# Conditioning chunks 5 to 24 computed between the projection units of layer 0

## The reference

```
mod     = silu(c)     @ ada_w[i] + ada_b[i]      # 1 x 6144, ada_w[i] is 1024 x 6144
mod_ctx = silu(c_ctx) @ ada_w[i] + ada_b[i]
sh1, sc1, gt1, sh2, sc2, gt2 = split(mod, 6)
z = modulate(rmsnorm(x, pre_mix_g), sh1, sc1) @ w_in       # 1024 x 1888
...                                                        # three mixers (MLA, pooling, RWKV-7), w_out
x = x + gt1 * rmsnorm(y, post_mix_g)
h = modulate(rmsnorm(x, pre_ffn_g), sh2, sc2)              # then the MoE, 64 experts
x = x + gt2 * rmsnorm(f, post_ffn_g)
```

## Time and profile before

| | us |
|---|---|
| median of 3 runs (lowest, highest) | 2706.94 (2706.51, 2714.57) |
| the profiled execution, time | 2704.16 |
| its span, first to last instruction | 2702.3 |
| TensorE busy | 2199.4 (81%) |
| VectorE busy | 866.5 (32%) |
| mean granted clock of TensorE | 0.904 |

### The profile page before, as it was taken

How to read it: one execution, slowest core, us unless ns; L and a number is a source line. 1 busy time by engine, 2 the same in 40 slices (tenths; PEclk the granted TensorE clock), 3 DMA queues, 4 the chain that set the end, 5 groups by cost and what they waited for, 6 DMA issues and landing times. The chain is left out here.

```text
span 2702.3 us, 40433 instructions
## 1 busy us (share of the span) xinstructions
PE 2199.4 (81%) x15579; PEld 1215.5 (45%) x15579; DVE 866.5 (32%) x1930; ACT 347.5 (13%) x716; POOL 382.8 (14%) x563
## 2 busy tenths in 40 slices
PE   7999888778866888888996497877775999899990
PEld 1124465666435444444443244566533444444440
DVE  0220146675472111111111632567543111111113
ACT  0001232110220011011110013211020111111110
POOL 0000100000100222222221101000001222222220
PEclk9999989997976999899998699799786999999995
DMA  9890100003104999999994811000305999999983
GB/s 337 310 324 9 46 1 1 2 2 129 48 16 181 380 377 376 352 389 358 382 379 182 327 54 47 1 2 3 138 23 217 386 375 373 383 378 370 369 317 118
DMA packets 150297, 571.69 MB, mean 212 GB/s; under 512 B 26327, under 2 KB 36439, under 8 KB 116248
## 3 DMA queue, kind: packets, MB, share of 16 engines
q1 hardware_dynamic: 125600, 532.14, 51.9%
q0 software_dynamic: 24576, 37.82, 4.1%
HBM read 569.75 MB, written 46.24 MB: 228 GB/s over the span
## 5 line engine op out<-in xcount | busy, mean ns | idle before, releaser
L1137 PE MATMUL pb<-arena 128*64 128x256 f32 x3072 | 353.0, 380 | 15.1 <-DMA arena<-in_exp_w_down_dram 14.7
L1134 PE MATMUL pb<-arena 128*128 128x512 f32 x512 | 270.0, 686 | 98.8 <-DMA arena<-in_exp_w_down_dram 96.3
L1137 PEld LDWEIGHTS pb<-arena 128*64 128x64 f32 x3072 | 214.5, 134 | 135.7 <-issue 35.9
L1938 DVE TENSOR_TENSOR arena<-arena,pb 128x128 f32<-128x128 f32 (+1 forms) x128 | 41.1, 321 | 691.2 <-ACT arena L1403 691.2
L1982 POOL TENSOR_TENSOR arena<-arena 128x8 f32<-128x8 f32 (+1 forms) x44 | 74.7, 1698 | 1132.9 <-DVE arena L1439 643.3
L698 PE MATMUL pb<-arena 128*128 128x128 f32 x1136 | 156.2, 281 | 94.9 <-DVE arena L1447 68.0
L1134 PEld LDWEIGHTS pb<-arena 128*128 128x128 f32 x512 | 109.7, 220 | 239.1 <-issue 234.7
L720 PE MATMUL pb<-arena 128*128 128x480 f32 (+1 forms) x512 | 207.1, 566 | 2.3 <-ACT arena L1220 2.3
L698 PEld LDWEIGHTS pb<-arena 128*128 128x128 f32 x1136 | 127.8, 144 | 156.7 <-issue 152.8
L1152 PE MATMUL pb<-arena 128*64 128x512 f32 x768 | 186.0, 604 | 1.5 <-DVE arena L1944 1.5
L690 PE MATMUL pb<-arena 128*2 128x512 f32 x384 | 169.3, 602 | 18.8 <-DMA arena<-in_ada_w_dram 18.8
(11 more groups left out here) (291 smaller groups left out, 2678.1 us busy)
## 6 DMA issues: line engine op xcount, KB each, us to landing
arena<-in_exp_w_gate_dram SPq DMA_DIRECT2D x128, 1024.0 KB, 9.7
arena<-in_exp_w_up_dram SPq DMA_DIRECT2D x128, 1024.0 KB, 12.2
arena<-in_exp_w_down_dram SPq DMA_DIRECT2D x128, 1024.0 KB, 17.0
arena<-in_ada_w_dram SPq DMA_DIRECT2D x24, 2048.0 KB, 9.1
arena<-y_rows SPq DMA_DIRECT2D x36, 512.0 KB, 6.0
arena<-mod_rows SPq DMA_DIRECT2D x21, 512.0 KB, 8.5
arena<-in_w_out_dram SPq DMA_DIRECT2D x8, 1024.0 KB, 8.4
arena<-in_w_in_dram SPq DMA_DIRECT2D x4, 1920.0 KB, 16.8
```

The costliest lines, as they stand in the source:

```text
L1134: last = mm(pb[:, 2 + j % 2, :], gT[:, j % 2, k, :], ring_gu[:, j, :, k, :], start=(k == 0), stop=(k == KD - 1))
L1137: last = mm(pb[f * FEW:(f + 1) * FEW, 2 + j % 2, 0:FF], gT_few[:, j % 2, k, :], ring_gu[:, j, :, k, f * P:(f + 1) * P], start=(k == 0), st ...
```

## The change

Only the rows sh1 and sc1 of layer 0 (four chunks, in the order 2, 3, 0, 1) are computed ahead of the projection, from four buffers of their own. `w_in` of layer 0 is loaded right behind them. The other 20 chunks are loaded one at a time into the space of `mix`, in two halves of 1 MB, and multiplied behind the units of layer 0's projection, 5 chunks for every 4 units (`ada_after`). A chunk's products no longer accumulate in one pair of rows: k-slice k goes to the column group k mod 4, 32 columns wide (2 used, the others zero), so that four partial sums stand at partitions 0, 32, 64 and 96. ScalarE copies the 128 x 512 bank to SBUF, and one more matmul with a 0/1 matrix (`fold`) adds the four. VectorE then makes the finished half row of the chunk (`mod_add`), with the gain where there is one, and it is stored on its own: by ScalarE's queue for the first four, which also issues the four broadcast loads, by SyncE for the others. Squares and roots of all four token tiles of layer 0 are made at once, ahead of the first norm. The MLA weights of layer 0 are loaded when the last row is stored. All tile turns use banks 0 and 1, since 2 and 3 hold the partial sums.

```diff
+    parts["fold"] = (t[:, None] % 32) == np.arange(2)[None, :]
...
+        first_ada = Region(arena, R0, R2).take(4 * KD * 512).rearrange("p (j k n) -> p j k n", j=4, k=KD)
+        ada_ring = mix.rearrange("p i d -> p (i d)").rearrange("p (h k n) -> p h k n", h=2, k=4)
...
+        mod_row = r.take(4 * 512).rearrange("p (j n) -> p j n", j=4)
+        gain_row = r.take(512)
...
+        ADA = [(0, c) for c in (2, 3, 0, 1, 4, 5, 6, 7, 8, 9, 10, 11)] + [(1, c) for c in (2, 3, 0, 1, 4, 5, 6, 7, 8, 9, 10, 11)]
+        N_ADA = len(ADA)
+        ada_after = lambda n: range(4 + n * (N_ADA - 4) // (4 * NT), 4 + (n + 1) * (N_ADA - 4) // (4 * NT))
...
+            return {1: "pre_mix_g", 2: "post_mix_g", 4: "pre_ffn_g", 5: "post_ffn_g"}.get(ADA[n][1] // 2)
...
+                l, c = ADA[n]
+                own = slice(c * 512, (c + 1) * 512)
+                sp.dma_start(mod_row[0:2, n % 4, :], A["ada_b"][l:l + 1, own].broadcast_to([2, 512])).then_inc(ada_rows_in, 16)
+                if ada_gain(n):
+                    of = slice(c % 2 * 512, (c % 2 + 1) * 512)
+                    sp.dma_start(ada_gain_at(n), A[ada_gain(n)][l:l + 1, of].broadcast_to([2, 512])).then_inc(ada_rows_in, 16)
...
+            def mod_store(q, n):
+                l, c = ADA[n]
+                q.wait_ge(ada_row, n + 1)
+                q.dma_start(mod_dram[l][:, c * 512:(c + 1) * 512], mod_row[0:2, n % 4, :]).then_inc(mod_out, 16)
+            def ada_stream(chunks):
+                for n in chunks:
+                    l, c = ADA[n]
+                    w = A["ada_w"][l].rearrange("(p k) n -> p k n", p=P)[:, :, c * 512:(c + 1) * 512]
+                    for h in range(2):
+                        sp.wait_ge(ada_part, 2 * n - 1 + h)
+                        sp.dma_start(ada_ring[:, h], w[:, 4 * h:4 * h + 4, :]).then_inc(ada_in[h], 16)
+                    if n > chunks[0]:
+                        mod_store(sp, n - 1)
+                    sp.wait_ge(mod_out, 16 * n)
+                    ada_rows(n)
+            def ada_last(n):
+                mod_store(sp, n)
+                sp.wait_ge(mod_out, 16 * (n + 1))
...
-            for n in range(12 * DEPTH):
-                l, c = n // 12, n % 12
-                if n >= NA:
-                    sp.wait_ge(ada_sum, n + 1 - NA)
-                sp.dma_start(ada_ring[:, n % NA], A["ada_w"][l].rearrange("(p k) n -> p k n", p=P)[:, :, c * 512:(c + 1) * 512]
-                             ).then_inc(ada_in[n % NA], 16)
...
-                        load_bc(0, 1)
-            for c in range(4):
+            sp.dma_start(cst, A["shape_consts"]).then_inc(start_in, 16)
+            for n in range(4):
+                l, c = ADA[n]
+                sp.dma_start(first_ada[:, n], A["ada_w"][l].rearrange("(p k) n -> p k n", p=P)[:, :, c * 512:(c + 1) * 512]).then_inc(ada_in[n], 16)
+                ada_rows(n)
+            sp.dma_start(x[:, 0:NL, :], A["x"].rearrange("a (i p) d -> p (a i) d", p=P)).then_inc(tokens_in, 16)
+            load_w_in(0, 0)
+            sp.dma_start(x[:, NL:NT, :], A["ctx"].rearrange("a (i p) d -> p (a i) d", p=P)).then_inc(tokens_in, 16)
+            for c in range(1, 4):
                 load_w_in(0, c)
-            mod_store(DEPTH - 1)
+            ada_stream(range(4, N_ADA))
+            ada_last(N_ADA - 1)
...
+                    g = k % 4
+                    last = mm(pb[32 * g:32 * g + 32, 2 + n % 2, :], cs[:, k, :], w[:, g, :], start=(k < 4), stop=(k >= 4))
+                return last
+            def ada_main(n):
+                pe.wait_ge(ada_row, n - 1)
+                for h in range(2):
+                    pe.wait_ge(ada_in[h], 16 * (n - 2))
+                    ada_products(n, ada_ring[:, h], range(4 * h, 4 * h + 4)).then_inc(ada_part, 1)
+            def ada_fold(n):
+                pe.wait_ge(ada_copy, n + 1)
+                mm(pb[0:2, 2 + n % 2, :], c_("fold"), mod_part[:, n % 2, :], start=True, stop=True).then_inc(ada_sum, 1)
...
-            pe.wait_ge(ada_row, 12 * DEPTH)
+            for n in range(4):
+                if n >= 2:
+                    pe.wait_ge(ada_row, n - 1)
+                pe.wait_ge(ada_in[n], 16)
+                ada_products(n, first_ada[:, n, 0:4, :], range(4)).then_inc(ada_part, 1)
+                ada_products(n, first_ada[:, n, 4:8, :], range(4, 8)).then_inc(ada_part, 1)
+                if n == 0:
+                    pe.wait_ge(start_in, 16)
+                else:
+                    ada_fold(n - 1)
+            ada_fold(3)
+            pe.wait_ge(ada_row, 4)
...
                     pe.wait_ge(h_ready, seen(h_ready))
-                    turn_tile(hbuf[:, i % 2, :], 2 * (i % 2)).then_inc(hT_sum, 1)
...
                         n += 1
                         if c == 2 and i + 1 < NT:
                             h_turn(i + 1)
+                        for a in ada_after(n - 1) if l == 0 else ():
+                            ada_main(a)
+                            if a > 4:
+                                ada_fold(a - 1)
+                if l == 0:
+                    ada_fold(N_ADA - 1)
+                    pe.wait_ge(ada_row, N_ADA)
...
+            act.wait_ge(cs_zero, 1)
+            ac(cs[:, :, 0:2].rearrange("p k s -> p s k"), craw, ACT.Silu).then_inc(silu_c, 1)
+            def ada_copied(n):
+                act.wait_ge(ada_part, 2 * n + 2)
+                if n >= 2:
+                    act.wait_ge(ada_sum, n - 1)
+                ac(mod_part[:, n % 2, :], pb[:, 2 + n % 2, :], ACT.Copy).then_inc(ada_copy, 1)
+            for n in range(4):
+                ada_copied(n)
+            for n in range(4):
+                act.wait_ge(ada_row, n + 1)
+                act.dma_start(mod_dram[0][:, ADA[n][1] * 512:(ADA[n][1] + 1) * 512], mod_row[0:2, n % 4, :]).then_inc(mod_out, 16)
+            act.wait_ge(mod_out, 64)
+            for s in range(2):
+                for a in range(2):
+                    act.dma_start(bc[:, 2 * s + a, :], mod_dram[0][s:s + 1, (1 - a) * D:(2 - a) * D].broadcast_to([P, D])).then_inc(bc_in[s], 16)
             for l in range(DEPTH):
                 def turned(i):
                     act.wait_ge(hT_sum, seen(hT_sum))
-                    ac(hT[:, :, i * P:(i + 1) * P], pb[:, 2 * (i % 2):2 * (i % 2) + 2, :].rearrange("p b (k t) -> p (b k) t", k=4), ACT.Copy
+                    ac(hT[:, :, i * P:(i + 1) * P], pb[:, 0:2, :].rearrange("p b (k t) -> p (b k) t", k=4), ACT.Copy
                        ).then_inc(hT_ready, 1)
                 turned(0)
-                if l == 0:
-                    act.wait_ge(mod_rows, DEPTH)
...
                             turned(i + 1)
+                        for a in ada_after(4 * i + c) if l == 0 else ():
+                            ada_copied(a)
                 end_phase(act, "act")
                 act.wait_ge(mla_in, seen(mla_in, 64))
...
-                for c in range(12):
-                    dve.wait_ge(ada_sum, 12 * l + c + 1)
-                    part = modrow[0:2, c * 512:(c + 1) * 512]
-                    last = V.tensor_tensor(part, pb[0:2, (12 * l + c) % 8, :], part, ALU.add)
-                    last.then_inc(ada_row, 1)
-                dve.wait_ge(ada_row, 12 * (l + 1))
-                def mr(j):
-                    return modrow[0:2, j * D:(j + 1) * D]
-                V.scalar_tensor_tensor(mr(1), mr(1), 1.0, pre_mix_row[0:2, :], ALU.add, ALU.mult)
-                V.tensor_tensor(mr(2), mr(2), post_mix_row[0:2, :], ALU.mult)
-                V.scalar_tensor_tensor(mr(4), mr(4), 1.0, pre_ffn_row[0:2, :], ALU.add, ALU.mult)
-                V.tensor_tensor(mr(5), mr(5), post_ffn_row[0:2, :], ALU.mult).then_inc(mod_rows, 1)
-                dve.wait_ge(mod_rows, sent(mod_rows))
-                if l == 0:
+            def mod_add(n):
...
+                dve.wait_ge(ada_rows_in, 16 * sum(2 if ada_gain(a) else 1 for a in range(max(n + 1, 4))))
+                dve.wait_ge(ada_sum, n + 1)
+                own, gain, part = mod_row[0:2, n % 4, :], ada_gain_at(n), pb[0:2, 2 + n % 2, :]
+                j = ADA[n][1] // 2
+                if ada_gain(n):
+                    step(V.tensor_tensor(own, part, own, ALU.add))
+                if j in (1, 4):
+                    V.scalar_tensor_tensor(own, own, 1.0, gain, ALU.add, ALU.mult).then_inc(ada_row, 1)
+                elif ada_gain(n):
+                    V.tensor_tensor(own, own, gain, ALU.mult).then_inc(ada_row, 1)
+                else:
+                    V.tensor_tensor(own, part, own, ALU.add).then_inc(ada_row, 1)
+                dve.wait_ge(ada_row, sent(ada_row))
+            for n in range(4):
...
+                mod_add(n)
+            dve.wait_ge(tokens_in, 32)
+            for s in range(2):
+                for i in range(NL * s, NL * s + NL):
+                    step(V.tensor_tensor_reduce(htmp, x[:, i, :], x[:, i, :], 1.0, 0.0, ALU.mult, ALU.add, ssq[:, i:i + 1]))
+            inv_root(ssq[:, 0:NT], D, EPS)
+            for i in range(2):
...
```

(51 more changed lines are left out.)

19 lines of the change are left out of this document (4 added, 15 removed).

## The result

The changed kernel takes 2758.23 us (median of 4 runs, 2756.23 to 2761.04) against 2706.73 for the kernel before: ratio 1.0181, 95% interval [1.0167, 1.0194]. It is slower by 51.5 us. The forecast was 2780 with a range of 2745 to 2820. The table gives marks of the two profiled executions, in us from the first instruction.

The account below looks back on a forecast made before the run. The first stage was TensorE-bound; the changed one a serial load-to-store chain. Start, 18 cycles of 15.3 us (275) and end put MLA's first turn at 373 instead of 299.69: 73 us more, 2780 against the median, range 2745 to 2820.

Parts of the forecast that it names:

- the store is not in the cycle: Streamed chunks: loads do not wait for the row store, cycle 9.4 us, kernel faster at 2674 us; chance 0.06.
- The store: Streamed chunk's cycle: SyncE's 4 KB row store and its wait, taken as 2.6 us between bounds 1.9 and 3.3.
- Load: Streamed chunk's cycle: 2 MB with nothing in flight lands in 8.3 us, plus 0.1 from landing to start.
- Products: Streamed chunk's cycle: the second half's 8 matmul instructions on four column groups, 1.0 us, bounds 1.0 and 3.4.
- The clock: Stream: TensorE's clock falls at four long gaps and a little elsewhere, adding 0.6 us per cycle.
- Start: Ahead of the stream: early chunks, stores, broadcasts and first norm, with the projection's unit 0 starting at 57.5 us.
- end at 34.5: Start: the last early chunk's products, copy, fold and addition are done at 34.5 us, after landing at about 30.
- Chunk 4 is the later one: Start of the stream: chunk 4 lands at 66 us, after unit 0 starts at 57.5; its products end at 68.
- End: After chunk 23 lands at 352: last rows and stores to 364.5, then 8.4 us of MLA weights, turn at 373.
- Four signs: Expected trace marks: TensorE idle 5 to 6 us a cycle, first unit before 60, last after 340, MLA turn after 365.
- Groups in turn: Chunk products: the four column groups run one after the other, 3.4 us instead of 1.0, kernel 2840 us; chance 0.08.
- Low clock throughout: Stream: clock stays low, products and fold 4 instead of 2 us, cycle 16.9 us, kernel 2807 us; chance 0.12.

Follow-up runs that it names:

- experiment 1: The changed kernel with SyncE storing the row of chunk n-2 instead of n-1, so the next load does not wait for it: 2679.53 us, 0.990.
- the filler: The changed kernel with extra f32 matmuls, their result overwritten, put ahead of TensorE's wait for each chunk load: 2750.72 us, 1.0169.
- Experiment 7: The changed kernel with the bias and gain rows of the first four chunks issued ahead of the constants and chunks: 2757.59 us, 1.0189.
- experiment 5: The changed kernel with the four MLA loads of layer 0 moved ahead of the stream, behind w_in: 2750.70 us, 1.0165.

## Why the prediction was right, and where it was off

*The bound.* Right. The stream is a chain through load, products, fold, addition, store and rows. Taking links out gave 79 us back, doubling one cost 27, both as that chain says (80 and 23 were expected). The rival "the store is not in the cycle" was priced at 2674, and the kernel in which that is made so took 2679.5. That nearness is in part luck: the rival's 9.4 us a cycle were a load and a second half, while in experiment 1 TensorE's own work fills the cycle of 9.5 except where two chunks stand together.

*The size.* 53 us against 73 in the spans, and the terms that were off can be read one by one:

- The store was put at 2.6 us, midway between a 4 KB load and the 48 KB store; it took 1.23 with its issue. 1.4 by 18 is 25 us, more than the whole miss. The nearer end would have been a better choice than the middle: 4 KB against 48 is a reason, and a write against a load had none in the rows.
- Load: 8.0 us to the start of the second products instead of 8.4, 7 us in all.
- Products 0.88 instead of 1.0, fold 1.02, additions 1.56 instead of 1.4, rows as forecast.
- The clock: 0.6 a cycle was forecast. At full clock a cycle with a gain took 13.24, and the mean of all, a third of them shorter by one addition of 0.7, was 14.0: 1.0 us, of which the filler took back 0.7, with 4 of the 18 folds still long. That is 7 us too little in the sum, in the other direction.
- Together the cycle was 14.0 instead of 15.3: 23 us less.
- Start: 64.8 instead of 57.5. The step that failed is that products, copy, fold and addition of the last early chunk "end at 34.5": I had taken the bias rows as free, and they queue behind the chunks on SyncE's list. The last addition ended at 41.6. Experiment 7 takes 6.0 us of it away. Row 4 was stored at 85.7 where the forecast has 79.7, 6 us more. "Chunk 4 is the later one" failed too: its products ran at 73.06, right behind the first unit, without a wait for the load.
- End: 15.1 us from the store of row 22 to the turn instead of 17.6, the two stores again.
- A slip without effect: the lower values given for the terms add up to 13.15 us, not to the 12.9 of the text.

6 - 23 - 2.5 is -19.5 us: 373 forecast, 352.8 measured. So the store alone was 25 us too long, and the start and the clock, 13 us too short, hid half of that.

*The signs.* SyncE's waits came as forecast: 20 for a row, and 20 for the stores (19 at line 532, one at 574). The loads are 14.0 us apart in the mean, but 8 of the 18 distances lie under 14. The clock was below full. Four signs did not come: TensorE idle on the loads for 4.4 us a cycle and not 5 to 6, the first unit at 64.8 and not before 60, the turn at 352.8 and not after 365, and the last unit at 307.31 and not after 340. The last one did not even fit the forecast's own sum: two chunks stand behind that unit, so at 15.3 us each it would have begun near 323.

*The rivals.* Groups in turn: no, 182.0 against 70.3 us; priced at 2840, measured 2836 when made so. Low clock throughout: no, but it fell in more than half of the cycles, and not only at the long gaps. The MLA weights stood bare at the end and cost 5.6 us there (experiment 5).

*What the text had as a rival only* is how near the change was to a gain: it gives the kernel with the store outside the cycle a chance of 0.06, and not as an edit to make. The same edit with the store one chunk later is 26 us faster than the kernel before.

## What to carry to other kernels

When a load is moved under other work, follow the issuing queue's program order round one full turn: what the queue waits for between two loads is part of the load's period, even if it has nothing to do with the buffer. Here fold, additions, a 4 KB store and the rows' issues took the distance between loads from about 9.5 to 14.0 us, while TensorE and the DMA engines both had time to spare (0.68 and 0.41 busy). Judge an edit of one stage by a marker at that stage's end when the rest of the program varies by more than the edit is worth.

## What the runs showed of the hardware that I had not expected

- A 4 KB store of two rows was done 1.2 us after its issue, where a 48 KB one of two rows took 3.3. In experiment 1, with a chunk's load in flight, it took 4.6 us on average.
- Four groups of 32 columns carried 8 instructions of 512 in 0.88 us from the first start to the fold's, 0.11 us each, where one group needs 0.43.
- Adding 51.8 us of matmuls to a stage made it 8.9 us shorter, with a granted clock of 0.95 instead of 0.83. No single idle time decides when it falls. At 207.99 (2.25 us idle before) the first half's products took 1.54 us and the second half's 1.94 instead of 1.06; at 225.31 the second half's took 1.79, with 1.59 and 1.50 us idle before the two halves, and at 305.48 they took 1.06 with 1.41 and 1.50. Yet the earlier trace rows had 3.00 us without a fall, behind 30 us of unbroken work of TensorE.
- A DMA of one bias row, issued right behind a 2 MB load at the start, held SyncE for 4.3 to 5.3 us in three of four cases (1.15 behind the first load), where it takes 0.25 in the stream. Why was not tested. The changed kernel's queue of SyncE:

```profile
4.34 0.56 SPq L582 DMA_DIRECT2D arena<-in_ada_w_dram  x1
4.94 4.27 SPq L532 DMA_DIRECT2D arena<-in_ada_b_dram  x1
...
14.59 0.55 SPq L582 DMA_DIRECT2D arena<-in_ada_w_dram  x1
15.18 5.28 SPq L532 DMA_DIRECT2D arena<-in_ada_b_dram  x1
```
